# Five more turns of gate and linear projections by seven block products in place of eight

## The reference, cut to what matters

```
g, u = split(h @ w_gu, 2)          # gate and linear projections, 1024 -> 2 x 2816
y = (silu(g) * u) @ w_dn           # down projection, 2816 -> 1024
```

## Time and profile before

| | us |
|---|---|
| median of 3 runs (2270.97 to 2274.76) | 2272.86 |
| the profiled execution | 2272.57 |
| its span, first to last instruction | 2270.8 |
| PE busy | 2232.8 |
| DVE busy | 1269.7 |
| ACT busy | 954.6 |
| POOL busy | 1154.1 |

### The profile page before, as it was taken

The page is one execution under the profiler, slowest core; times in us unless marked ns, Lnnn a source line. Parts: engine busy times, 40 slices in busy tenths (PEclk is TensorE's granted clock), DMA queues, the critical chain, the costliest instruction groups (busy, mean ns, idle before and its releaser), DMA issues.

```text
span 2270.8 us, 34984 instructions
## 1 busy us (share of the span) xinstructions
PE 2232.8 (98%) x11158; PEld 1870.7 (82%) x11158; DVE 1269.7 (56%) x2039; ACT 954.6 (42%) x1740; POOL 1154.1 (51%) x892
## 2 busy tenths in 40 slices
PE   8999999999999999999999999999999999999997
PEld 7888888888888888888998778888677787888996
DVE  6899785626733525755344335555565557755442
ACT  4334663323322333433553354444665454333552
POOL 3455555444444454544885443333322455544984
PEclk9999999999999999999999999999999999999999
DMA  4333444337746532549663233334311432549661
GB/s 153 96 97 97 144 121 158 93 117 259 282 144 210 202 93 74 167 166 319 202 196 94 80 86 111 111 108 132 113 52 52 152 94 74 185 161 316 203 187 59
DMA packets 184536, 327.00 MB, mean 144 GB/s; under 512 B 18096, under 2 KB 59184, under 8 KB 183664
## 3 DMA queue, kind: packets, MB, share of 16 engines
q1 hardware_dynamic: 163040, 278.46, 40.1%
q10 hardware_dynamic: 21392, 47.23, 5.5%
HBM read 291.96 MB, written 33.55 MB: 143 GB/s over the span
## 4 chain that ended last, share of the span: by engine, by line
PE 88%; DVE 6%; issue 3%; ACT 2%; POOL 1%; DMA 0%; ACTq 0%; DVEq 0%; POOLq 0%
PE bank L1275 22%; PE bank L1277 22%; PE bank L1276 22%; PE bank L1431 3%; PE bank L1433 3%; PE bank L1432 3%; PE bank L1598 2%; PE bank L1600 2%; PE bank L1599 2%; PE bank L1688 1%; PE bank L1651 1%; PE bank L1732 1%; POOL wlo L556 1%; PE bank L1754 1%; DVE bank L2121 1%
## 5 line engine op out<-in xcount | busy, mean ns | idle before, releaser
L556 POOL TENSOR_TENSOR wlo<-raw,whi 128x512 fp32r<-128x512 f32 (+1 forms) x830 | 1082.1, 1317 | 1017.1 <-ACT whi L660 1015.1
L660 ACT ACTIVATE whi<-raw 128x512 fp32r<-128x512 f32 (+1 forms) x830 | 506.8, 617 | 620.1 <-PE bank L1277 454.9
L1275 PE MATMUL bank<-a_hi,whi 128*128 128x512 f32 x1608 | 637.3, 396 | 6.5 <-POOL wlo L556 2.7
L1277 PE MATMUL bank<-a_lo,whi 128*128 128x512 f32 x1608 | 626.2, 389 | 0.0
L1276 PE MATMUL bank<-a_hi,wlo 128*128 128x512 f32 x1608 | 625.9, 389 | 0.0
L1275 PEld LDWEIGHTS bank<-a_hi,whi 128*128 128x128 f32 x1608 | 301.9, 188 | 76.2 <-issue 6.8
L1277 PEld LDWEIGHTS bank<-a_lo,whi 128*128 128x128 f32 x1608 | 301.8, 188 | 63.5
L1276 PEld LDWEIGHTS bank<-a_hi,wlo 128*128 128x128 f32 x1608 | 302.1, 188 | 62.8 <-issue 1.4
L1275 PE MATMUL bank<-b_hi,whi 128*128 128x512 f32 x852 | 335.2, 393 | 1.7 <-DVE b_lo L1953 1.1
L1277 PE MATMUL bank<-b_lo,whi 128*128 128x512 f32 x852 | 332.0, 390 | 0.0
L1276 PE MATMUL bank<-b_hi,wlo 128*128 128x512 f32 x852 | 332.0, 390 | 0.0
(11 more groups left out here) (311 smaller groups left out, 2768.6 us busy)
## 6 DMA issues: line engine op xcount, KB each, us to landing
raw<-d_stream SPq DMA_DIRECT2D x750, 256.0 KB, 2.7
G<-d_ada SPq DMA_DIRECT2D x72, 512.0 KB, 4.7
G<-d_stream SPq DMA_DIRECT2D x80, 256.0 KB, 4.6
raw<-spill_rv SPq DMA_DIRECT2D x64, 256.0 KB, 3.0
spill_rv<-sq ACTq DMA_DIRECT2D x44, 256.0 KB, 4.6
spill_rv<-tmp ACTq DMA_DIRECT2D x32, 256.0 KB, 2.1
G<-spill_rv ACTq DMA_DIRECT2D x8, 1024.0 KB, 8.3
spill_rv<-G ACTq DMA_DIRECT2D x20, 256.0 KB, 5.0
```

Source lines behind the costliest of these rows:

```text
L556: pool.tensor_tensor(wlo[:, s % SRING, c], raw[:, s % RING, c], whi[:, s % SRING, c].bitcast(F32), ALU.subtract).then_inc(lo_done, 1)
L660: act.activation(whi[:, p % SRING, c], raw[:, p % RING, c], ACT.Copy).then_inc(hi_done, 1)
L1275: pe.matmul(out_ps, w_hi, hi[:, k, :], start=first and q == 0, stop=False)
L1277: mm = pe.matmul(out_ps, w_hi, lo[:, k, :], start=False, stop=last and q == len(ks) - 1)
```

## The change

Layers 2 and 3 get a product stage `wg{n}a` between `gu{n}a` and `dn{n}a`: three turns in layer 2 and two in layer 3, so `gu2a` keeps 3 plain turns and `gu3a` 4. The sums for both product stages of a layer (64 and 56) are made at places that a table lists, each with its stage, panel and number: beside `dn1a` 16, `gu1b` 4, `dn1b` 8, `gu2a` 4, `dn2a` 32, and for layer 3 beside `dn2b` 8, `wout` 8, `gu3a` 8, `dn3a` 32. In `dn2a` and `dn3a` every third panel has two sums. The rings keep four given and three made slots; sums made before `gu2a`, in `dn2b` and in `wout` use three other slots. The turned operands are ready one turn earlier: parts 1 and 2 both in turn 1, part 3 in turn 2. The core of the diff:

```diff
-PRODUCTS = {"wg2b": 5, "wg3b": 5}
-PLAIN_TURNS, MADE_PER_TURN = 2, 4
+PRODUCTS = {"wg2a": 3, "wg2b": 5, "wg3a": 2, "wg3b": 5}
 GIVEN_RING, MADE_RING = 4, 3
...
+MADE_AT = [(2, "dn1a", x, 1) for x in range(8, 24)] + [(2, "gu1b", x, 1) for x in range(33, 40, 2)] \
+    + [(2, "dn1b", x, 1) for x in range(1, 16, 2)] + [(2, "gu2a", x, 1) for x in range(17, 24, 2)] \
+    + [(2, "dn2a", x, 2 if x % 3 == 2 else 1) for x in range(24)] \
+    + [(3, "dn2b", x, 1) for x in range(1, 16, 2)] + [(3, "wout", x, 1) for x in range(7, 15)] \
+    + [(3, "gu3a", x, 1) for x in range(17, 32, 2)] + [(3, "dn3a", x, 2 if x % 3 == 2 else 1) for x in range(24)]
...
+            def load_beside(stage, lo, hi):
+
+                for p in range(lo, hi):
+                    load(p, 0, 0, -sums_before(p))
+                    for t in made_beside(stage, p - PLAN[stage][0]):
+                        given_load(t)
...
+            def given_load(t):
+
+                n, m = MADE[t][:2]
+                if t >= GIVEN_RING:
+                    sp.wait_ge(sums_made, t - GIVEN_RING + 1)
+                if MADE[t][2] == "wout":
+                    sp.wait_ge(opb, FILL_B["merged"] + KD)
...
+            def made_store(stage, x):
+
+                for t in made_beside(stage, x):
+                    act.wait_ge(sums_made, t + 1)
+                    act.dma_start(made_home(*MADE[t][:2]), made_place(t)).then_inc(made_out[t % MADE_RING], 16)
...
                 for x in range(5):
                     tick(name, i, x, 1)
-                    if i >= PLAIN_TURNS and x:
-                        made_store(n, m0 + x - 1)
-                if i < 4:
-                    turn_hi(b, i)
+                    if x:
+                        made_store(name, 8 * i + 2 * x - 1)
+                    if i == 1 and x == 2:
+                        turn_hi(b, 1)
+                if i < 3:
+                    turn_hi(b, i + 1)
...
+                    for i in range(1, plain_turns(n)):
                         made_turn(n, i)
...
+                    products_gates(f"wg{n}a", 2 * plain_turns(n))
                     made_down(n)
...
                 for half, K in (("a", FA), ("b", FB)):
-                    down = f"dn{n}{half}"
+                    name, down = f"wg{n}{half}", f"dn{n}{half}"
                     if half == "a":
-                        wide_stage(f"gu{n}a", OPA, opa, fill, FA // 2, late=n == 3)
...
+                        wide_stage(f"gu{n}a", OPA, opa, fill, plain_turns(n), late=n == 3)
+                    with pe.Fori(0, PRODUCTS[name]) as i:
+                        products_pair(name, i, 0, down)
+                        products_pair(name, i, 1, down)
...
+                dve.wait_ge(given_landed[t % GIVEN_RING], 16 * (t // GIVEN_RING + 1))
+                if t >= MADE_RING:
+                    dve.wait_ge(made_out[t % MADE_RING], made_out_at(t - MADE_RING))
...
+                for i in range(1, plain_turns(n)):
+                    for x in range(8):
+                        panel_sums(a, 8 * i + x)
+                    if i == 1:
+                        turn_values(fill, b, 1)
+                        turn_lo(b, 1)
+                    if i < 3:
+                        turn_values(fill, b, i + 1)
                     gate_pair(a, i, 0, at)
-                    if i < 4:
-                        turn_lo(b, i)
+                    if i < 3:
+                        turn_lo(b, i + 1)
                     gate_pair(a, i, 1, at)
...
             for m in range(KD):
+                panel_sums("wout", 2 * m)
+                panel_sums("wout", 2 * m + 1)
                 cross(1, "wout", m)
```

More of the change, by code:

```diff
@@ L120, in sums_before, with made_beside, made_index, made_out_at @@
     return n
[L123 to L138, removed]
+MADE_AT = [(2, "dn1a", x, 1) for x in range(8, 24)] + [(2, "gu1b", x, 1) for x in range(33, 40, 2)] \
[3 more added lines that the diff above has]
+    + [(3, "gu3a", x, 1) for x in range(17, 32, 2)] + [(3, "dn3a", x, 2 if x % 3 == 2 else 1) for x in range(24)]
+MADE, _count = [], {2: 0, 3: 0}
+for _n, _stage, _x, _many in MADE_AT:
+    for _ in range(_many):
+        MADE.append((_n, _count[_n], _stage, _x))
+        _count[_n] += 1
+assert all(_count[n] == 8 * (PRODUCTS[f"wg{n}a"] + PRODUCTS[f"wg{n}b"]) for n in (2, 3))
+MADE_LATE = ("gu2a", "dn2a", "gu3a", "dn3a")
+def made_beside(stage, x):
+    return [t for t, (_, _, at, s) in enumerate(MADE) if at == stage and s == x]
+def made_index(n, m):
+    return next(t for t, (block, k, _, _) in enumerate(MADE) if (block, k) == (n, m))
+def made_out_at(t):
+    return 16 * (t // MADE_RING + 1)
 def runs_of(lo, hi):
@@ L525, in _ @@
             ada_run("gu1a", 0, 6)
-            load_run(a + 48, b - a - 48)
+            load_beside("dn1a", a + 48, b - 8)
+            load_run(b - 8, 8)
             ada_run("gu1b", 6, 3)
             at = b + 24
[L529 to L538, removed]
+            for stage, n in (("gu1b", 1), ("dn1b", 1), ("gu2a", 2), ("wg2a", 2), ("dn2a", 2), ("wg2b", 2), ("dn2b", 2),
+                             ("wout", 3), ("gu3a", 3), ("wg3a", 3), ("dn3a", 3), ("wg3b", 3)):
+                first, _, panels, _ = PLAN[stage]
+                if stage == "wout":
+                    load_run(at, first - at, -sums_before(at))
+                    at = first
+                if stage in PRODUCTS:
+                    products_run(stage)
+                else:
+                    load_beside(stage, max(at, first), first + panels)
+                at = first + panels
             load_run(at, NUNITS - at, -sums_before(at))
@@ L700, in packed_tick @@
             def packed_tick(name, m, K):
-                lo, hi = -(-m * K // 4), -(-(m + 1) * K // 4)
-                tick(name, 0, lo, hi - lo)
+                for x in range(-(-m * K // 4), -(-(m + 1) * K // 4)):
+                    tick(name, 0, x, 1)
+                    made_store(name, x)
             def wide_tick(name, i, j, begun=0):
@@ L1247, in _ @@
             for m in range(KD):
-                tick("wout", 0, 2 * m)
+                for x in (2 * m, 2 * m + 1):
+                    tick("wout", 0, x, 1)
+                    made_store("wout", x)
                 wait_used(act, "wout", 0, 2 * m + 1)
@@ L1968, in seven_products @@
                 a, b, at = f"gu{n}a", n - 2, FILL_B[f"ffn{n}a"]
+                late = next(t for t, (_, _, stage, _) in enumerate(MADE) if stage == a)
+                for t in range(late - MADE_RING, late):
+                    dve.wait_ge(made_out[t % MADE_RING], made_out_at(t))
                 turn_values(fill, b, 0)
@@ L2035, in ffn @@
                             gate_pair(name, ada_turns, 1, at)
-                        with dve.Fori(ada_turns + (1 if ada_turns else 0), turns) as i:
+                        for i in range(ada_turns + (1 if ada_turns else 0), turns):
+                            for x in range(8):
+                                panel_sums(name, 8 * i + x)
                             for pr in range(2):
```

144 lines of the change are left out of this document (80 added, 64 removed).

## The result

| | us |
|---|---|
| kernel before beside it, median of 4 runs (2270.97 to 2274.76) | 2272.64 |
| changed kernel, median of 4 runs (2332.08 to 2335.57) | 2334.33 |
| ratio, 95% interval | 1.027 (1.0252 to 1.0288) |
| profiled execution of the changed kernel, its span | 2334.59, 2332.8 |

The change costs 61.7 us. The forecast was 2310 in a range of 2278 to 2335: the sign, the place and the mechanism were right, the size was 24 us short and all but at the upper end of the range.

The account below looks back on a forecast made before the run. The prediction took PE, busy 98% of the span, as the bound. From 2272.6 us it took 9.1 for the turns and added 43.8 for dn2a and dn3a, 1 for wout and 2 for the operands: 2310 us, range 2278 to 2335.

Parts of the forecast that it names:

- The turns: Five gate turns in blocks 2 and 3 become product turns, 19.94 us in place of 21.76: -9.1 us of PE.
- The sign it named: PE spends 80 to 95 us from dn2a's first matmul to wg2b's fourth panel, likewise in block 3.
- The start of dn2a: With S the stage's start on PE, ACT rounds panel 6 at S+19.0.
- The period: Loop of stores, sums and loads in dn2a and dn3a: 9.9 us per three panels, between 8.5 and 11.7.
- The tail: After dn2a's panel 24 at S+78.4, last sums and store landings delay wg2b's panel 3 to S+90.9.
- wout: Two sums before a tile's copy exceed DVE's gap for three tiles: 0 to 3 us late, 1 taken.
- its sign of a mis-sized term: PE waiting in wout or turn 1 of gu2a for more than 3 us means the small terms were mis-sized.
- The turned operands: Turn 1 computes two operands in place of one: 0 to 4 us per block, 2 us taken for both.
- A: Rival: queues keep up in dn2a and dn3a, only gain and small terms stand: 2266.5 us, chance 0.13.
- B: Rival: bandwidth is the bound in dn2a and dn3a, period near 8.5 us: 2294 us, down to 2274, chance 0.25.
- C: Rival: landings grow with fuller queues, period 11.7 us or more, early stages add delays: 2341 us, chance 0.10.

Follow-up runs that it names:

- e5: Changed kernel with the eight sums beside wout left out, the sums before them read again: 2325.6 us, ratio 1.0229.
- e9: Changed kernel with four further turns in place of five and sums spread so hardly any panel carries two, slots and load order kept: 2279.0 us.
- e10: As e6, but the 32 sums beside dn2a and dn3a are done by panel 20: 2286.4 us, ratio 1.0063.
- e6: Changed kernel with five made slots in place of three and, in dn2a and dn3a, given loads issued behind the raw load three panels further: 2298.7 us.
- e3: Changed kernel with given loads of panel x in dn2a and dn3a issued behind the raw load of panel x+3, same bytes: 2312.0 us.
- e4: Changed kernel with five made slots in place of three, same bytes and load order: 2305.3 us, ratio 1.0143.
- e8: Changed kernel with four further turns, e6's slots and load order, sums spread, 12 beside dn2b, 24 beside dn3a, none beside wout: 2272.9 us.

## Why the prediction was right, and where its size was off

**The turns.** 1.82 us less of PE for each, as said. e5 makes the gain visible: from pb to dn3a, without the sums beside wout, 229.57 us against 232.77, 3.2 of the 3.6 us that two turns are worth.

**The sign it named.** It wanted 80 to 95 us from the first matmul of dn2a to the fourth panel of wg2b, in both blocks. It was 99.4 in block 2 (1114.17 - 1014.75) and 99.5 in block 3, so this sign too says: the mechanism, but larger. ACT's waits were mostly the raw landings that it named (58.5 us), with 2.7 us for the landed stores.

**The start of dn2a.** Panel 6 was forecast at S+19.0 and came at S+17.8 (1032.58 - 1014.75).

**The period: the step that failed.** It was put at 9.9 us, "slightly below the middle" of 8.5 and 11.7, with the reason that a loop bound by latency thins the traffic. The traffic did thin, to 278 GB/s, but the landings hardly shortened: the medians of the transfers issued from 1028 to 1064 are

```profile
G<-d_stream SPq DMA_DIRECT2D x12, 256.0 KB, 3.7
raw<-d_stream SPq DMA_DIRECT2D x10, 256.0 KB, 4.0
spill_rv<-sq ACTq DMA_DIRECT2D x10, 256.0 KB, 4.1
spill_rv<-G ACTq DMA_DIRECT2D x5, 256.0 KB, 4.5
```

against 4.8 for raw loads and 4.3 for stores before. A likely reason, not tested by a run: several transfers still start together (five from 1051.5 to 1053.7, of which four took 4.5 to 5.0 us to land), and a mean over 40 us doesn't show that. The periods ranged from 9.66 to 13.02 us, with a mean of 11.27. Followed through the trace turn by turn, the six turns have on the mean 4.3 us for the store to land, 0.3 until it is issued and the sum begins, 1.8 for the sum (1.1 or 2.1 to 2.2, the longer ones with one add of 1.25 to 1.5 us), 0.45 to the raw issue and 4.35 for its landing: 11.2. The forecast had these very pieces for panel 6, 4.3 + 2.0 + 0.45 + 4.0 = 10.75, and then took a period below their sum, because it averaged a whole turn of the loop, 11.7, with a time by bandwidth, 8.5, that isn't a turn of the loop. Six periods at 1.37 us too little are 8.2 us a block: 16.4 of the 24 missing.

**The tail** was forecast at 12.5 us from panel 24's rounding to PE's fourth panel of wg2b and measured 14.0 (1100.17 to 1114.17). Its mechanism is the one given, in that it hangs on the last sums: e9 and e10 end the sums three panels earlier, and the loss in wg2b is gone. Which part is ACT's programmed wait for the last landing and which the copy behind the last store isn't separated; in e6 the landing alone held ACT 7.9 us. Together: -1.2 + 8.2 + 1.5 on 21.9 is 30.4 for block 2, and the borders give 30.8.

**wout** was put at 1 us and cost 6. The forecast set two sums against DVE's idle gap of 3.2 us. What it missed is that ACT has each pair of sums to store ahead of the tile's copy, in its program's order, so sum, store, copy and the norm's work become one chain per tile. The timeline of ACT in the changed kernel, the copies of three tiles in wout:

```profile
1895.60 0.60 ACT L1309 ACTIVATE G<-bank 128x512 f32<-128x512 f32 x1 [2.86 <-DVE G L1991]
...
1901.58 0.39 ACTq L759 DMA_DIRECT2D spill_ga<-G  x1
1902.01 0.60 ACT L1309 ACTIVATE G<-bank 128x512 f32<-128x512 f32 x1 [0.43 <-DVE G L1991]
...
1908.58 0.60 ACT L1309 ACTIVATE G<-bank 128x512 f32<-128x512 f32 x1 [0.36 <-PE bank L1336]
```

6.4 and 6.6 us from copy to copy, where PE needs 5.44 for a tile. The norm behind wout makes PE wait for it (L1437, 3.3 us once, and 1.5 on POOL's `tmp`), more than the 3 us that the forecast named as its sign of a mis-sized term. But PE's waits between pb and dn3a add up to 6.7 us against 3.9 before, which is less than half of the 6. The rest has the size of the clock: over 25 us around this norm its granted mean is 0.80 (1915 to 1940), where before had 0.93 (1885 to 1910) and e5 0.86 (1910 to 1935), and 0.13 of 25 us is up to 3.3. e5 takes 5.8 us of the 6 away, so both parts come from the sums beside wout. That is 5 of the missing 24.

**The turned operands** in gu2a and gu3a, dn1a and dn1b: 2 us forecast for both blocks. From the start of gu2a to dn2a the changed kernel takes 127.4 us, where 131.0 less three turns' gain is 125.6: 1.9 lost, and the experiments have 127.4 to 127.8 there. 0.4 is left in e5 between pb and dn3a (229.57 against 232.77 - 3.64), which the clock there (above) would cover. So about 2 in all, as forecast. The other 0.6 of the 2.5 us ahead of dn2a lies before gu2a, where the profiles reach gu2a at 883.7 to 887.3 us (886.7 before). No run separates the 1.9 by cause; PE's waits there are 0.6 us on POOL's low part and 0.7 on DVE's `tmp`.

**The rivals.** A (the queues keep up) fell in this kernel, but the reason given against it did not stand: "no window here held more than some 330 GB/s for long" is true of the kernel before for stretches of 40 us (at most 333), but its own trace has 429 GB/s from 349 to 359, and e6 held 366 GB/s for 40 us. The limit of about 358 GB/s that the prediction took from the Trainium skill (DMA: Bandwidth & Descriptors, Bandwidth) is passed there. The Trainium skill (HBM Reference, Specifications) says that a core streaming alone measures well above that share, and with that e6 agrees. B (bandwidth is the bound) fell by e3, e4 and e6. What came was the forecast's mechanism with a period near C's (11.3 us, where C had 11.7 or more).

## What to carry to other kernels

When a stage streams through small rings, write down which event frees which slot and how many steps of the bound engine the loop spans. One more sum on every third panel here shortened the span from 5 panels to 3, and a latency of some 11 us that had cost nothing became 11 us for every 8.16 of PE. Read a whole turn of the loop off the trace and use it as it is, and try two more slots or another issue order before believing that bandwidth is the bound. Work whose last product is stored and then waited for should end some panels before the stage does; and work put beside a stage that "has a gap" has to be followed through each in-order engine that handles it, not only through the one that computes it.

## What the runs showed of the hardware that was not expected

**The clock can fall in unchanged code, in one kernel and not in another.** The middle took 562.3 to 562.8 us in five profiled executions, 565.9 to 566.0 in five, and 563.7 and 564.8 in two. e8 comes to it 4.2 us earlier than the kernel before and loses 3 us in one place. The windows there of before and of e8, at the same instructions within 0.2 us:

```profile
1305.00:1314.00 9.00, 9.00 (x33) 5.87 (x32) 0.00 (x0) 2.99 (x5) 2.88 (x3) 1.00 0.19 58
```

```profile
1301.00:1310.00 9.00, 9.00 (x21) 5.28 (x20) 0.00 (x0) 1.78 (x3) 1.40 (x2) 0.64 0.21 58
```

The granted clock is 0.64 on the mean instead of 1.00, and matmuls of 512 columns start 0.43 us apart (1.2 GHz) instead of 0.23. In both kernels PE had just done a row of eight matmuls on 16 rows of the array; only in one did the clock fall. The five long middles are the profiles that have it for 6.8 us at this place (in e6 the granted clock is 0.50 from 1316.8 to 1323.6), e3 and e9 have it for 3.4 us, the other five not at all. When the place is reached doesn't sort them: e4 and e6 come to the middle within 0.8 us of each other, and it fell in e6 alone. So why it falls isn't settled, nor how often the executions without a profile have it. It has the size of what e8 won, so a gain of 0.15% in this kernel can't be read off a median alone.

**A PE that has waited often comes back slower.** In the changed kernel the granted clock is 0.84 from 1090 to 1101 and 0.87 from 1110 to 1120, around stalls of up to 6.4 us:

```profile
1090.00:1101.00 11.00, 9.79 (x36) 7.82 (x36) 5.15 (x12) 2.38 (x4) 3.85 (x4) 0.84 0.75 242
1110.00:1120.00 10.00, 9.46 (x70) 9.26 (x70) 0.00 (x0) 4.35 (x8) 7.18 (x7) 0.87 0.45 134
```

The clock stood at half there from 1092.1 to 1095.5, behind a wait of 2.2 us, and from 1105.7 to 1112.5, within and behind the wait of 6.4. It isn't so behind each wait: after 2.9 us up to 1079.9 it stayed full (1.00 from 1079.9 to 1085.0). In this block it cost next to nothing, for ACT waited for landings and sums there and not for PE, and from its fourth panel on wg2b took 96.4 us, 0.2 more than the 96.2 before. Behind wout it can have cost up to 3.3 us (above).
